# Two weight tiles placed 32 bytes further on in SBUF, the activations left in place

## The reference, cut to what matters

```python
def _swiglu(h, w_in, w_out):              # w_in: 1024 x 5632, w_out: 2816 x 1024
    gate, up = jnp.split(h @ w_in, 2, axis=-1)
    return (jax.nn.silu(gate) * up) @ w_out

x = x + 0.5 * _swiglu(_rms(x, norm_gain[layer, 0]), ffn_w_in[layer, 0], ffn_w_out[layer, 0])
h = _rms(x, norm_gain[layer, 1])
x = x + mixer(h)        # gated linear recurrence, dilated attention,
                        # stick-breaking attention, sliding-window attention
x = x + 0.5 * _swiglu(_rms(x, norm_gain[layer, 2]), ffn_w_in[layer, 1], ffn_w_out[layer, 1])
```

## The kernel before, in words

| tile | starts at | remainder by 64 |
|---|---|---|
| raw | 16,512 | 0 |
| whi | 41,088 | 0 |
| wlo | 63,616 | 0 |
| shift (not used by anything, 32 bytes) | 86,144 | 0 |
| x | 86,176 | 32 |
| xg | 94,368 | 32 |
| xk_hi, xk_lo | 110,752 and 118,944 | 32 |
| shift_rest (not used, 96 bytes) | 127,136 | 32 |
| cst (constant matrices) | 127,232 | 0 |
| hT | 147,104 | 32 |
| working tiles of the mixers, oT pairs among them | from 147,104 on | 32 |

## Time and profile before

### The profile page before, as it was taken

One profiled execution on the slowest core, in us unless ns is written; L12 is line 12 of the kernel. 1 busy time (PEld: TensorE's weight loads), 2 busy tenths in 40 slices (PEclk: granted clock), 3 DMA queues, 4 the chain that ended last, 5 costly groups with the idle time before them and its releaser, 6 DMA issues.

```text
span 2222.7 us, 39159 instructions
## 1 busy us (share of the span) xinstructions
PE 2170.6 (98%) x13971; PEld 1964.6 (88%) x13971; DVE 1619.0 (73%) x1932; ACT 1290.6 (58%) x1754; POOL 596.1 (27%) x483
## 2 busy tenths in 40 slices
PE   8999998999999999999999999999999999989998
PEld 7888998888888899999888888999888888878887
DVE  7876877886786676666887687645886788586873
ACT  5654655665665556665665566454665466445663
POOL 3421662341242000000342243100341244022430
PEclk9999989999999999999999999999999999999999
DMA  6665743666567555554566566544566566533662
GB/s 213 189 208 185 235 148 96 189 196 201 161 195 223 157 174 152 150 158 148 168 191 208 161 193 211 163 141 135 171 195 213 157 190 205 170 106 123 189 215 97
DMA packets 371155, 387.89 MB, mean 175 GB/s; under 512 B 11334, under 2 KB 366031, under 8 KB 371056
## 3 DMA queue, kind: packets, MB, share of 16 engines
q1 hardware_dynamic: 357104, 369.14, 53.7%
q10 hardware_dynamic: 13952, 17.41, 2.5%
HBM read 376.02 MB, written 10.49 MB: 174 GB/s over the span
## 4 chain that ended last, share of the span: by engine, by line
PE 87%; DVE 8%; ACT 2%; issue 1%; POOL 1%; DMA 0%; ACTq 0%; POOLq 0%; DVEq 0%
PE ps L806 43%; PE ps L807 23%; PE ps L760 3%; PE ps L761 3%; PE ps L762 3%; DVE wlo L1621 2%; PE ps L917 1%; PE ps L781 1%; DVE xg L1639 1%; PE ps L782 1%; PE ps L783 1%; PE ps L850 1%; PE ps L852 1%; PE ps L851 1%; DVE hg_E L1752 1%
## 5 line engine op out<-in xcount | busy, mean ns | idle before, releaser
L1621 DVE TENSOR_TENSOR wlo<-raw,whi 128x1024 fp32r<-128x1024 f32 (+2 forms) x652 | 884.6, 1368 | 144.9 <-ACT whi L1236 144.0
L806 PE MATMUL ps<-xg,whi 128*128 128x512 f32 x2816 | 981.5, 392 | 4.1 <-DVE wlo L1621 2.3
L1236 ACT ACTIVATE whi<-raw 128x1024 fp32r<-128x1024 f32 (+2 forms) x652 | 721.0, 1113 | 203.6 <-PE ps L807 131.1
L807 PE MATMUL ps<-xg,wlo 128*128 128x256 f32 x2816 | 795.3, 282 | 0.0
L806 PEld LDWEIGHTS ps<-xg,whi 128*128 128x128 f32 x2816 | 529.2, 188 | 117.1 <-DVE xg L1639 3.3
L807 PEld LDWEIGHTS ps<-xg,wlo 128*128 128x128 f32 x2816 | 534.1, 190 | 0.2
L806 PE MATMUL ps<-hT,whi 128*128 128x512 f32 x1408 | 488.5, 390 | 0.0
L807 PE MATMUL ps<-hT,wlo 128*128 128x256 f32 x1408 | 397.5, 282 | 0.0
L806 PEld LDWEIGHTS ps<-hT,whi 128*128 128x128 f32 x1408 | 264.3, 188 | 55.0
L807 PEld LDWEIGHTS ps<-hT,wlo 128*128 128x128 f32 x1408 | 266.8, 189 | 0.0
L2142 POOL TENSOR_TENSOR gate_r<-gate,r 128x512 f32<-128x512 f32 x88 | 189.6, 2154 | 287.3 <-DVE gate L1699 287.3
(11 more groups left out here) (260 smaller groups left out, 3082.1 us busy)
## 6 DMA issues: line engine op xcount, KB each, us to landing
raw<-in_ffn_w_in SPq DMA_DIRECT2D x352, 512.0 KB, 3.5
raw<-in_ffn_w_out SPq DMA_DIRECT2D x64, 768.0 KB, 5.1
raw<-in_ffn_w_out SPq DMA_DIRECT2D x64, 640.0 KB, 5.1
raw<-in_w_kv SPq DMA_DIRECT2D x48, 512.0 KB, 3.8
raw<-in_a_w_in SPq DMA_DIRECT2D x32, 512.0 KB, 4.6
raw<-in_b_w_q SPq DMA_DIRECT2D x24, 512.0 KB, 4.0
raw<-in_sb_w_qkv SPq DMA_DIRECT2D x24, 512.0 KB, 4.6
bias_by_distance<-bias_rows ACTq DMA_DIRECT2D x12, 768.0 KB, 4.4
```

The source lines that it names most:

```text
L806: nc.tensor.matmul(out, whi[:, par, w], both, start=first and k == 0, stop=False)
L807: mm = nc.tensor.matmul(out[:, 0:T], wlo[:, par, w], both[:, 0:T], start=False, stop=last and k == total - 1)
L1236: nc.scalar.activation(whi[:, par, off:off + size], raw[:, 2 * par + half, :size], ACT.Copy).then_inc(hi_done, 1)
L1621: nc.vector.tensor_tensor(wlo[:, par, off:off + size], raw[:, 2 * par + half, :size], whi[:, par, off:off + size].bitcast(F32), ALU.subtra ...
```

## The change

The 32 unused bytes that stood behind `wlo` now stand ahead of `whi`:

```diff
     raw = sb("raw", [P, 4, HALF])
+    ahead = sb("ahead", [P, 8])
     whi = sb("whi", [P, 2, SLOT], F32R)
     wlo = sb("wlo", [P, 2, SLOT], F32R)
-    shift = sb("shift", [P, 8])
     x = sb("x", [P, KC, T])
     xg = sb("xg", [P, KC, 2, T], F32R)
```

## The result

The changed kernel takes 2243.29 us (median of 4 runs, 2243.22 to 2249.24), the kernel before 2219.55 us (median of 4 runs). The ratio is 1.0108, with a 95% interval of 1.0096 to 1.0120: 24 us slower.

The account below looks back on a forecast made before the run. The prediction took TensorE, with matmuls filling 98% of the span, as the bound, so only their pitch could move the time. Stationary weight loads added 16 us, all other terms 0: 2220.35 + 16 = 2236 us, range 2218 to 2262.

Parts of the forecast that it names:

- Step 1: Weights as stationary operand in wide matmuls and projections, phase 0 to 32: 1.4 ns on each of 11,568 loads, +16 us.
- rival C: Stationary and moving operands at the same phase disturb each other: +42 us, 2264 us; chance 0.20 with its lesser forms.
- Step 2: Weights as moving operand in the value slots, phase 0 to 32: 0 for 1008 matmuls, bounds +1.7 and −1.7 us.
- Step 3: ScalarE and VectorE write and read whi and wlo at phase 32, raw still at 0: hidden under TensorE, 0.
- A: The phase of stationary operands is free, as the load runs beside the matmul: no change, 2220 us; chance 0.20.
- B: A moving operand at phase 0 slows the value slots, and the change mends it: −1.7 us, 2218.7 us; chance 0.13.
- D: A lucky interleaving takes 1.2 ns off each wide matmul: −10 us, 2210 us; chance 0.05.

Follow-up runs that it names:

- e1_both_0: Against the kernel before, unused bytes put all weights and activations at phase 0 (address by 64), distance 0 by 128; 1.0088 of before.
- e6_distance_64: Against the kernel before, weights in place and every activation 32 bytes further on, so the distance is 64 by 128; 1.0096 of before.
- e7_both_plus32: Against the changed kernel, weights in place and every activation 32 bytes further on, so all distances are those of before; 0.9998 of before.
- e5_only_wlo: Against the kernel before, only wlo moved to phase 32 (distance 0 by 128), whi and activations in place; 1.0011 of before.
- e11_lo96_hi32: Against the kernel before, activations 128 bytes further on, distance by 128 still 32 from whi but 96 from wlo; 1.0127 of before.
- e8_distance_160: Against the kernel before, weights in place and every activation 128 bytes further on, distance 32 by 128 but 160 by 256; 2219.89 us in one run.

## Why the prediction was right, and where it wasn't

**The bound.** That only the pitch could move the time held: idle time ahead of L806 3.6 for 4.1 us, TensorE at 98% in both.

**Step 1, the sum.** I had +16 us with 1.4 ns a load, measured were +24 us. The term was mis-sized and its reason wrong. I read the value slots' extra 1.4 ns as the price of a stationary operand at phase 32. e1_both_0, e6_distance_64 and e7_both_plus32 refute that from both sides. The value slots have the same distance by 128 as the input projections, with the roles exchanged; why they take up to 1.7 ns more no run shows. What holds instead: the wide pair has 6.7 ns more in six blocks of eight, 5 ns on average or 2.5 a load; the input projections have about 3 ns a matmul. The price of 2.8 and 5 ns that I had read from L1065 and L965, L966, rival C, was the better guide to the mechanism, since both of their operands have the phase that the changed kernel gives to all. As a price it was too high: 42 us assume 7.8 ns in every pair.

By the sign that I had named myself, a wide pair that grows by 5 ns and more, the case is C's and not my forecast's: six blocks of eight grew by 6.7 ns. 2243.29 us is also the very end of the forecast's own range, 2225 to 2243. Slower was right, but for a reason that does not hold, and the time lies inside the whole range because C was counted into it. In so far the number was luck.

**Rival C** came nearest, but "equal phases disturb" is not the rule either: distances 64 and 96 are slow as well. My sentence against it said that the rows were few and rounded. They were (six pitches in the earlier trace rows, not seven), but they were also the only rows with the distance in question: in the built program `dl_blk` and the two `dl_sq` tiles lie 4096 and 2048 bytes apart, `sk_ident` and `sk_mask` 512, so 0 by 128, as the weights and activations after the change. That was a reason for more than 0.20.

**Step 2, the value slots.** Predicted unchanged at 118.3, measured 120.0 ns, at the bound that I gave (+1.7 us for 1008 matmuls).

**Step 3.** The splits' medians moved by 3 and 1 ns. As predicted, nothing.

**Rivals A, B and D.** A, the address is free: refuted. Both places of the Trainium skill that spoke for it fall short here. By "SBUF — State Buffer", Specifications, the lines have 16 bytes, so a move by 32 crosses as many as before. The pitch changed all the same, from 346.7 to 353.3 ns. By "TensorE: Matmul & The Clock Gate", Step-by-step, the weight load has a read port of its own and takes no read bandwidth from the moving operand. Yet the pitch here depends on the distance between just these two. B, a moving operand at phase 0 is slow: the value slots' moving operand left phase 0 and they became slower, and in e7_both_plus32 `xg` moves at phase 0 at full speed. D, a lucky interleaving: not in the changed kernel, but it exists (344.4 ns in e5_only_wlo, 113.3 ns in e6_distance_64).

**What is shown, and what is not.** Shown: the loss follows the distance between the stationary and the moving tile, not the place of either; it is there in windows at full clock; and it doesn't depend on the engines that write the weights. For the last I sorted the wide matmuls with `hT` by what else was busy when they started. From the start of L806 to the next matmul it was 228.4 ns both in 343 cases where VectorE, ScalarE and GpSimd all stood still and in 119 where all three worked; in the changed kernel it was 235.0 ns in 357 and 234.9 ns in 108 such cases. Not shown is the mechanism inside. The weight load starts together with the running matmul, and two streams of reads from SBUF that get in each other's way, more or less as their addresses meet, would fit the distance, the repeating pattern and its dependence on how a block starts. No run observed the reads themselves, so this stays a guess. Nor is there a rule that gives the pitch from the two distances.

## What to carry to other kernels

When TensorE is full, measure the pitch (first to last start over a few hundred matmuls, divided by their count) and compare it between stages of the same form: it shows losses of one or two per cent that busy times and waits don't. Such a loss can hang on the distance in SBUF between the tile that is stationary and the tile that moves; so an unused 32 bytes between two tiles are part of a kernel's speed, and any new tile allocated between the two can cost 1%, as here, with no wait that shows it. Try a few distances by unused bytes, each with several runs, and distrust a gain that comes with more scatter: it can be blocks falling into one pattern or another.

## What was unexpected of the hardware

- One program runs the same loop at two or three paces, each steady from the 25th pair of a block (the second in one) to its 528th: 346.7 or 353.3 ns in the changed kernel, 344.4, 346.7 or 353.3 ns in e5_only_wlo.
- The slow pace of the changed kernel is a repeating pattern, three pairs of 361, 349 and 350 ns. In e11_lo96_hi32 the same 353.3 ns come from equal pairs of 353 and 354 ns, and one fast block of the changed kernel alternates between 350 and 343 ns, so a pattern doesn't make a block slow.
- Two other matmuls in between could change the pace: one block of the changed kernel ran at 346.7 ns ahead of L818 and L819 and at 353.3 ns behind them.
- Two kernels that differ by 64 bytes in the place of `wlo` alone took 2219.89 us (e8_distance_160, one run) and 2248.06 us (e11_lo96_hi32), the latter 1.27% above the kernel before (1.10 to 1.43%).
- float32r matmuls of 256 columns with a new stationary operand each ran at pitches from 113.3 to 120.3 ns in kernels that differ in unused bytes alone.
